# Six seams of a two-block transformer kernel: waits bank by bank, decays a head ahead, an output product begun inside its attention, transposes hooked to other pieces

## What is computed

```python
# block 1, two layers; the mixer of layer 0 is "even", that of layer 1 "odd"
mix = even_mixer(x) if l == 0 else odd_mixer(x)      # see below
x = layer_norm(ALPHA * x + mix)
x = layer_norm(ALPHA * x + square(relu(x @ ffn_w1)) @ ffn_w2)     # 1024 -> 4096 -> 1024
x = x + sigmoid(x @ ple_w_gate) * rms_norm(p[l] @ ple_w_proj)

def even_mixer(x):                 # one input product, then two mixers side by side
    qa, ka, va, hq, hf, hi, hg = split(x @ w_in)
    return concat(diff_attention(qa, ka, va), hgrn2(hq, hf, hi, hg)) @ w_out

def hgrn2(...):                    # 4 heads of 128, chunks of 64 tokens
    b = cumsum(log f);  b_mid, b_last = b[31], b[63]          # per chunk
    a = tril((q * exp(b - b_mid)) @ (k * exp(b_mid - b)).T)
    o = a @ v + (q * exp(b)) @ state
    state = exp(b_last) * state + (k * exp(b_last - b)).T @ v

def odd_mixer(x): ...              # "dilated" attention, 16 heads of 64, causal with a mask of counts

# block 2, one layer
z = rms_norm(x) @ w_in             # q, k, v, su, sv, ga, gb
x = x + (sigmoid(ga) * gqa_attention(q, k, v) @ w_att_out
         + sigmoid(gb) * spatial_gating(gelu(su), gelu(sv)) @ w_sgu_out) @ w_out
x = x + cross_attention(rms_norm(x), rms_norm(mem)) @ w_co    # 4 heads of 128, 256 memory rows
x = x + moe(rms_norm(x))           # 16 experts, top 2, each 1024 -> 512 -> 1024
return rms_norm(x)
```

## Time and profile before

| | before |
|---|---|
| median of three runs | 2305.15 us (2304.0 to 2308.02) |
| the profiled execution, its own time | 2305.15 us |
| its span, first to last instruction | 2303.1 us |
| TensorE busy | 2215.6 us, 96% of the span |
| VectorE, ScalarE busy | 56%, 48% |
| mean granted TensorE clock | 0.986 of full speed |

### The profile page before, as it was taken

The page is one execution under the profiler, slowest core; times in us unless marked ns, Lnnn a source line. Parts: engine busy times, 40 slices in busy tenths (PEclk is TensorE's granted clock), DMA queues, the critical chain, the costliest instruction groups (busy, mean ns, idle before and its releaser), DMA issues.

```text
span 2303.1 us, 30060 instructions
## 1 busy us (share of the span) xinstructions
PE 2215.6 (96%) x10999; PEld 1811.4 (79%) x10999; DVE 1299.9 (56%) x1911; ACT 1107.0 (48%) x1642; POOL 52.5 (2%) x70
## 2 busy tenths in 40 slices
PE   9999999999999999999999999999999799999994
PEld 7887788888888876788888888868888678888883
DVE  4556663333374446653333467642554579899995
ACT  3425363433432238362432444473344278888884
POOL 1000000000000000000000000000000010000001
PEclk9999999999999999999999999999999799999997
DMA  6220233333323320243333333203222299999994
GB/s 194 83 74 28 83 119 93 99 96 95 101 74 101 92 74 1 92 129 100 92 100 95 97 101 99 89 20 101 88 86 82 71 379 411 411 412 412 411 409 187
DMA packets 129137, 338.57 MB, mean 147 GB/s; under 512 B 10528, under 2 KB 11712, under 8 KB 129040
## 3 DMA queue, kind: packets, MB, share of 16 engines
q1 hardware_dynamic: 117744, 296.85, 36.7%
q0 software_dynamic: 7840, 27.59, 3.6%
q10 hardware_dynamic: 3456, 12.81, 1.4%
HBM read 320.96 MB, written 16.25 MB: 146 GB/s over the span
## 4 chain that ended last, share of the span: by engine, by line
PE 88%; DVE 7%; ACT 3%; DMA 1%; issue 1%; POOL 0%; SPq 0%; DVEq 0%; ACTq 0%; POOLq 0%
PE bank L2271 42%; PE bank L2274 18%; PE bank L2681 11%; PE bank L2718 6%; PE bank L2344 2%; PE bank L2353 2%; PE bank L2410 1%; PE bank L2295 1%; DVE w_l L1345 1%; PE bank L2368 1%; PE bank L2661 1%; PE bank L2333 0%; ACT w_h L821 0%; DVE stat L1377 0%; PE bank L2668 0%
## 5 line engine op out<-in xcount | busy, mean ns | idle before, releaser
L1345 DVE TENSOR_TENSOR w_l<-w_raw,w_h 128x1024 fp32r<-128x1024 f32 x370 | 447.4, 1221 | 555.3 <-ACT w_h L821 551.7
L821 ACT CAST w_h<-w_raw 128x1024 fp32r<-128x1024 f32 x370 | 385.6, 1050 | 728.0 <-PE bank L2271 511.1
L2271 PE MATMUL bank<-w_h,xt_h 128*128 128x512 f32 (+1 forms) x960 | 376.4, 392 | 7.1 <-DVE w_l L1345 2.6
L2271 PE MATMUL bank<-w_h,xt_l 128*128 128x512 f32 (+1 forms) x960 | 371.4, 387 | 0.0
L2271 PE MATMUL bank<-w_l,xt_h 128*128 128x512 f32 (+1 forms) x960 | 371.0, 386 | 0.0
L2271 PE MATMUL bank<-w_h,ht_h 128*128 128x512 f32 x624 | 244.0, 391 | 0.7 <-DVE w_l L1345 0.7
L1345 DVE TENSOR_TENSOR w_l<-spare,w_h 128x1024 fp32r<-128x1024 f32 x184 | 220.5, 1218 | 41.6 <-ACT w_h L821 40.9
L2271 PE MATMUL bank<-w_h,ht_l 128*128 128x512 f32 x624 | 242.9, 389 | 0.0
L2271 PE MATMUL bank<-w_l,ht_h 128*128 128x512 f32 x624 | 242.8, 389 | 0.0
L2274 PE MATMUL bank<-xt_h,w_h 128*128 128x512 f32 x608 | 236.8, 389 | 3.4 <-ACT arena L961 2.4
L2274 PE MATMUL bank<-xt_h,w_l 128*128 128x512 f32 x608 | 236.6, 389 | 0.0
(11 more groups left out here) (351 smaller groups left out, 2908.4 us busy)
## 6 DMA issues: line engine op xcount, KB each, us to landing
w_raw<-in_ffn_w_dram SPq DMA_DIRECT2D x128, 512.0 KB, 3.7
spare<-in_w_down_dram SPq DMA_DIRECT2D x92, 512.0 KB, 10.9
spare<-in_w_gate_dram SPq DMA_DIRECT2D x88, 512.0 KB
w_raw<-in_w_up_dram SPq DMA_DIRECT2D x88, 512.0 KB, 11.0
w_raw<-in_w_in_dram SPq DMA_DIRECT2D x30, 512.0 KB, 3.7
w_raw<-in_ev_w_in_dram SPq DMA_DIRECT2D x28, 512.0 KB, 3.7
w_raw<-in_od_w_in_dram SPq DMA_DIRECT2D x24, 512.0 KB, 3.7
slot_y_dram<-slot_out ACTq DMA_DIRECT2D x23, 512.0 KB, 6.7
```

The costliest lines, as they stand in the source:

```text
L821: nc.scalar.copy(w_h[:, n % SLOTS, :], raw_of(n)).then_inc(sem("w_hi"), 1)
L1345: V.tensor_tensor(w_l[:, s_, :], raw_of(n), w_h[:, s_, :].bitcast(F32), ALU.subtract)\
L2271: mm = T.matmul(bank[set0 + m][:, 0:g.width], a[:, c, toks_of(m)], b[:, kk, :], start=first, stop=last)
```

## The change

1. hgrn: `decays(h + 1)` stands behind `states(h)`, a head ahead; the gain multiplication and the rotations stand behind the split of piece 1 and ahead of `masked(h)`, no longer between `decays` and `operands`.
2. The waits for `at_out` at the end of `attention` and `pairs` are gone. For the differential attention one stands in the output product, behind (1, 0), ahead of bank 6, which the attention's values used.
3. Cross attention gets the follower `c_o[0]`: at k = n TensorE waits for the last exponentials and for two transposed chunks of the output, and does piece 0 of `c_o[0]` (24 matmuls) ahead of the last transposes and values. Its `set0` values are written out.
4. Feed-forward: the wait for all banks of `proj` is gone. Round 0 is written out on TensorE (the loop does rounds 1 and 2) and its first groups wait for `proj`'s banks one by one. In layer 0 the first group uses the other set and doesn't wait for them at all.
5. Block 2: the transposes of tile 3 stand behind (1, 3) of `m2_q`, not (1, 2); `queries_transposed` stands behind (0, 3) of `m2_sv`, not (2, 2).

```diff
+        c_o[0].set0, c_o[1].set0 = 0, 4
...
                 if h:
                     split(g.n + LOOK, None, 0)
                     head_out(h - 1)
-                    decays(h)
-                    if h == 1:
-                        heads_g = HG.rearrange("p t (h d) -> p (t h) d", d=P)
-                        dve.wait_ge(sem("bank_free"), plan.freed[m0_hg.g][1])
-                        own.mark(V.tensor_tensor(heads_g, heads_g, hg_g.unsqueeze(1).to_broadcast([P, 16, P]), ALU.mult))
-                    elif h == 2:
-                        rope(m0_q, q_stage)
-                    else:
-                        rope(m0_k, k_stage)
                     operands(h)
                 split(g.n + LOOK + 1, None, 0)
+                if h == 1:
+                    heads_g = HG.rearrange("p t (h d) -> p (t h) d", d=P)
+                    dve.wait_ge(sem("bank_free"), plan.freed[m0_hg.g][1])
+                    own.mark(V.tensor_tensor(heads_g, heads_g, hg_g.unsqueeze(1).to_broadcast([P, 16, P]), ALU.mult))
+                elif h:
+                    rope(*((m0_q, q_stage) if h == 2 else (m0_k, k_stage)))
                 masked(h)
                 split(g.n + LOOK + 2, None, 0)
                 states(h)
+                if h < 3:
+                    decays(h + 1)
                 split(g.n + LOOK + 3, None, 0)
...
-            def product(g, i=None, js=None, tiles=False, then=None):
+            def product(g, i=None, js=None, tiles=False, then=None, freed_at=None):
...
                     if j == 0 and plan.before[g.g] is not None:
-                        if (tiles or g.banked) and i is None:
+                        if freed_at:
+                            pe.wait_ge(sem(freed_at[0]), freed_at[1] - 3 + m)
+                        elif (tiles or g.banked) and i is None:
...
-            def attention(name, steps, probs, pt, ot_src=None, extra=None):
+            def attention(name, steps, probs, pt, ot_src=None, extra=None, follower=None):
...
                     if extra:
                         extra(k)
-
-                pe.wait_ge(sem("at_out"), s0 + n)
+                    if follower and k == n:
+                        pe.wait_ge(sem("at_prob"), 2 * (s0 + n))
+                        pe.wait_ge(sem("ot_lo"), ot.start[name] + 2)
+                        product(follower, js=(0,))
+
                 if ot_src is not None:
                     pe.wait_ge(sem("ot_lo"), ot.start[name] + ot_chunks[name])
...
                         product(follower, js=(0,))
-                pe.wait_ge(sem("at_out"), s0 + n)
...
-                    product(outp[0], js=(0, 1), then={(1, 1): heads_transposed})
+
+                    product(outp[0], js=(0, 1), then={
+                        (1, 0): lambda: pe.wait_ge(sem("at_out"), un.start["diff"] + len(diff_steps)),
+                        (1, 1): heads_transposed})
...
                 product(proj[1], then={(0, 0): seam_tile(ln1, X, 3)})
-                all_free(proj[1].g)
-                with pe.Fori(0, NQ - 1) as i:
+
+                product(ffn[0], 0, freed_at=plan.freed[proj[1].g] if ffn[0].set0 == proj[1].set0 else None)
+                product(ffn[1], 0, freed_at=plan.freed[proj[1].g])
+                product(ffn[2], 0)
+                product(ffn[3], 0)
+                with pe.Fori(1, NQ - 1) as i:
                     for g in ffn:
                         product(g, i)
...
-            product(m2_q, tiles=True, then={(0, 1): seam_tile("m2", XN, 2), (1, 2): seam_tile("m2", XN, 3)})
+            product(m2_q, tiles=True, then={(0, 1): seam_tile("m2", XN, 2), (1, 3): seam_tile("m2", XN, 3)})
...
-            product(m2_sv, then={(2, 2): queries_transposed})
+            product(m2_sv, then={(0, 3): queries_transposed})
...
-            attention("cross", cross_steps, c_probs, c_pt, c_ot)
-            product(c_o[0])
+            attention("cross", cross_steps, c_probs, c_pt, c_ot, follower=c_o[0])
+            product(c_o[0], js=(1,))
```

## The result

The changed kernel takes 2287.94 us (median of 5 runs, 2285.06 to 2293.16) against 2305.15 (5 runs, 2302.95 to 2308.02): a ratio of 0.993, 95% interval 0.9912 to 0.9949. A second measurement gave 2288.90 against 2303.34, 0.994 (0.9927 to 0.9953). The profiled execution took 2285.06 us with a span of 2283.1; that is 20.0 us less than the span of before, of which about 13.4 are the seams, about 6 are stretches in which TensorE's clock was not halved this time, and 0.7 lie at the start and in the experts.

A forecast was written before the change was run, and what follows sets the result against it. TensorE was taken as the bound, busy 2215.6 of 2303.1 us, leaving 87.5 us to better ordering. Terms 4.3 + 1.2 + 1.9 + 2.9 + 1.4 + 1.0 + 0.45 = 13.15 off 2305.15 gave 2292.0 us, range 2287.0 to 2297.5.

The forecast's parts named there:

- hgrn: Three TensorE waits ahead of the scores go, 3.5 us plus 0.27 restart each: 4.3 us, bounds 0 and 4.4.
- rival 2: A late operand takes back the gain of hgrn and of the queries: 2297.3 us; chance 0.14.
- End of the differential attention: The 1.08 us wait ahead of the output product goes, with a small part of a restart: 1.2 us, bounds 0.8 and 1.4.
- `pairs`: Ends of two attentions: waits of 0.9 us each go, with a small part of a restart: 1.9 us, bounds 1.6 and 2.4.
- Feed-forward: Wait between `proj` and the first matmul goes, 1.19 plus 0.28 us restart in each of two layers: 2.9 us.
- Tile 3 and the queries: Block 2: later transposes save 1.4 us at `m2_q`, 1.0 at the queries, where the stall moves to `su`'s gelu.
- Cross attention: Follower removes one 0.37 us idle time and a restart; 0.37, 0.72 and 1.45 stay: 0.45 us, bounds 0 and 1.0.
- rival 3: Written-out round 0 exposes seven more instruction packets at 4.1 us each, costing 28.7: 2320.7 us; chance 0.03.
- the one on the clock: Behind the cross attention, the 1.7 us lost to the halved clock were left in, so not counted as gain.
- rival 1: The clock holds behind the cross attention, winning 1.7 us more: 2290.3 us; chance 0.16.

The follow-up runs named there:

- Experiment 3: Changed kernel with round 0 still written out, but the old wait for all banks of `proj` put back ahead of it: 2291.97 us.
- Experiment 4: Changed kernel with the queries' transposes back at their old place, behind (2, 2) of `m2_sv`: 2290.94 us.
- Experiment 8: Changed kernel with the follower in four slices and, on ScalarE, the gelu of `sv` ahead of a split of `su`: 2282.63 us, ratio to before 0.991.
- experiment 5: Changed kernel run again unaltered: 2288.90 us, median of 6 runs (2285.17 to 2293.58).
- experiment 2: Changed kernel with hgrn's decays back directly ahead of the operands; gain multiplication and rotations stay behind the split: 2292.57 us.
- experiment 7: Changed kernel with the cross attention's 24 follower matmuls cut into four slices of six: 2286.23 us, ratio to before 0.9923.
- experiment 1: Changed kernel with hgrn's gain multiplication and rotations back ahead of the operands; only the decays stay a head ahead: 2289.48 us.
- experiment 11: Changed kernel without the cross-attention follower, a repeat execution: 2288.80 us.

## Why the prediction was right, and where it was off

The forecast was 2292.0 us with a range of 2287.0 to 2297.5; both medians, 2287.94 and 2288.90, lie in it, 3 to 4 us under the forecast. The sum of the seams was right: 13.15 forecast, 13.05 + 0.32 measured.

- **hgrn**, 4.3: measured 4.38. The margin at `masked` was larger than feared, so rival 2, the late operand, didn't come. That restarts cost 0.27 each is confirmed: 3.5 us of idle time gave 4.38.
- **End of the differential attention**, 1.2: measured 1.45. I took "a small part of a restart"; it was a whole one, 1.10 + 0.28 = 1.38.
- **`pairs`**, 1.9: measured 1.97, in two halves of 0.98 and 0.99.
- **Feed-forward**, 2.9: measured 2.93, but the working was only two thirds right. I put all of 1.47 a layer down to the wait for the banks and its restart. Experiment 3 shows 0.5 of it to be the entry into the loop, which goes because the round is written out. The number held by luck, since both parts stand in the same gap of the earlier trace rows, and the edit removes both. What the per-bank waits would win with the loop left where it was, no run shows.
- **Tile 3 and the queries**, 1.4 and 1.0: measured 1.35 (1.54 to 0.19) and, from the total of 2.32, 0.97. That the stall moves on to the gelu of `su` was right to within 0.1 us: 1.36 measured, in the 1 to 1.5 named. Experiments 4 and 8 show it from both sides.
- **Cross attention**, 0.45: 0.32 up to the logits in the changed kernel and 0.35 on before; 0.44 if the routing's part is counted (61.15 and 61.16 against 60.72). The chain of links wasn't shortened.
- **Code that doesn't stream** (rival 3): seven packets more, as counted, and no idle time from them. By the rule of the Trainium skill ("Runtime: NRT & Kernel Launch", Instruction fetch mechanics), that straight code is fetched ahead, this was to be expected, and the trace agrees: every group of round 0 takes 43.52 us.

**The step that was off** is the one on the clock: "I leave that as it is, since the same idle times stand ahead of the next large product." The idle times do stand there, 0.72 and 1.40, and yet the clock held in all nine executions with the 24 matmuls ahead of them. This is rival 1, to which I gave 0.16, and its price of 1.7 us was right (1.65). With it the sum is 14.85 and the time 2290.3; where the prediction says of it that "the sum would be 1.7 us lower", it is the time that is lower. The Trainium skill's rule ("TensorE: Matmul & The Clock Gate", Part 1), that the gate looks at recent activity, was the better guide here: dense work in front of the same idle time kept the clock. Its other half, that the gate runs free of the program's start, agrees with experiment 5, where the same kernel fell at two places at which it had held before.

The longest stretches it doesn't explain: in all fourteen executions one of 20.5 to 27.3 us begins in the small matmuls of the routing's transposes and logits, with no idle time of TensorE over 0.15 us in the 14 us ahead of it.

**What is left.** The medians of the first measurement differ by 17.21 us, 2.4 more than 14.85; those of the second by 14.44, 0.4 less. The forecast is a time, counted from 2305.15; from the second median of before, 2303.34, the same sum gives 2288.5, and 2288.90 was measured. So that both medians lie under the forecast is in part the place of this starting point, and the rest I can only place in the clock. In the two profiled executions the stretches account for 0.64 us in the differential attention, 1.65 behind the cross attention, 2.07 in the routing and about 1.5 in the last products. Those at 201, in the routing and at 2266 are at places that the change doesn't touch. Other executions of the changed kernel fell at one or more of them (at the first in experiments 2, 3, 5 and 7, at the last in 1, 4 and 11), and both measurements have runs from 2285 to 2293.6, one kernel, 8 us apart. What a fall costs depends on what runs there: 1.65 us behind the cross attention, 1.5 in the grouped attention and in the last products, 0.6 to 1.3 in the differential attention. The runs above 2292 have a mean granted clock of 0.985 to 0.986 and those under 2288 one of 0.988 to 0.990; between 0.990 and 0.986 lie some 9 us of clock over the span (an estimate: 0.004 of 2290), enough for the 8. That it is the clock throughout was not shown for the runs without a trace. Whether the change makes falls rarer at places it doesn't touch, or moves them by chance, stays open: it would take many profiled executions of both.

## What to carry to other kernels

When a chain of short links ends a stage and independent work is at hand, put it in slices between the links, not in one block ahead of them: the same 24 matmuls gave 0.3 us in a block and 3.2 in four slices. When a hook is moved, ask what the next instruction on the same engine waits for: of the 2.4 us ahead of the queries 1.4 came back at `su`, and one reordered split on another engine took 0.95 of that away. Before a gap ahead of a loop is put down to a wait, read the "issue" piece behind the wait in the chain: that part is the entry into the loop, and here it went when the loop was entered behind 192 matmuls and no longer behind a wait. And compare kernels that differ by less than their runs spread by the distance between the same two instructions in both traces, up to a point ahead of any stretch at another clock.

## What the runs showed of the hardware

- TensorE's granted clock falls from 2.4 to 1.2 GHz for a stretch of 3.4 us, 24 times in the fourteen profiled executions, and each time at the end of an idle time of 1.35 to 2.45 us (2.45 ahead of the queries; 1.43 at the start of the differential attention; 1.35 at that of the grouped one; 1.40 or 1.45 behind the cross attention; 1.8 and 2.06 in the experts) or within 1.9 us behind it. A stretch costs up to 1.7 us, and 0.6 to 1.3 in the differential attention. The same kernel falls at such a place in one execution and not in the next. The longer stretches in the routing, 20.5 to 27.3 us, begin without an idle time.
- Entering the loop of the feed-forward rounds costs TensorE 0.5 us behind a wait (0.58 of "issue" against 0.09), and nothing to be seen behind 192 matmuls (at 477.70 in the changed kernel).
- A stop between large products costs about 0.28 us more than its idle time (43.80 against 43.52 us for 192 matmuls); ahead of the scores, 0.27 (1.16 against 0.89 for eight), and that even where hardly any idle time is seen, as in experiment 1.
